# First layer's attention: heads p and 4+p together in four steps, values stationary, probabilities scaled before they are turned

## The chip, the cores and the metric

The kernel runs on one core of a Trainium2 chip (trn2). The metric is the device time of one launch, in microseconds (us), as the median of three runs. TensorE (PE) multiplies matrices and writes PSUM; its weight loads are shown apart as PEld. VectorE (DVE), ScalarE (ACT) and GpSimd (POOL) work element by element; SyncE (SP) issues the DMAs. Each engine runs its own list of instructions in the order in which they are written, and the engines wait for each other on semaphores.

## The reference

256 tokens of 1024 features pass through two layers of one kind and one of another. Only the mixer of the first layer is touched:

```python
def even_mixer(y, w_in, w_out, sinks, lb, gnorm_w):
    qa, ka, va, qb, fb, ib, gb = jnp.split(y @ w_in, EVEN_SPLITS, axis=-1)
    qa, ka = rope(qa), rope(ka)             # 8 query heads of 64, 2 key/value heads of 64
    oa = chunk_band_attention(qa, ka, va, 2, None, sinks)
    ob = hgrn2(qb, fb, ib, gb, lb, gnorm_w)  # 4 heads of 128, recurrent over 8 blocks of 32 tokens
    return jnp.concatenate([oa, ob], axis=-1) @ w_out

# chunk_band_attention, with sinks, for query head h and key/value head h // 4
m = max(max(s), sink[h])
p = exp(s - m)
p = p / (sum(p) + exp(sink[h] - m))
o = p @ v
# hgrn2, from block to block
o = qd @ state
state = dec * state + ke.T @ vv
```

## The kernel before

**Weights.** The weights come as units of 128 x 1024 numbers. SP loads unit n into `raw` (L531), ACT rounds it to `hi` (`round_unit`, L617), DVE subtracts to get `lo` (`split_unit`, L1513), and TensorE multiplies hi*hi, hi*lo and lo*hi. `units(upto)` in the lists of ACT and DVE does this for all units up to a number; TensorE waits for `lo_done` in `wait_unit`. Every place at which a unit is split is written out by hand in the two lists.

**The stage that the change touches.** TensorE's loop L1242 to L1262 has eight steps, one for each attention head s. A step issues the scores of head s (`scores`, L1110, the keys' and queries' 64 rows as contraction, PSUM bank s % 2), a share of the filler (`fill`, L1187), the recurrence's products (`kv`, L1197), the mix of head s-1 (`mix`, L1133, turned probabilities stationary, 64 columns of values moving), and at last the turning of the probabilities of head s (`turn_probs`, L1122). The heads of key/value head 0 (s below 4) all lie on array rows 0 to 63, the others on rows 64 to 127.

**Filler.** `fill` computes three products of the same layer and of the memory (hg, mk, mv): 12 pieces i of 8 steps each, a step being 3 matmuls of 256 columns. Pieces 2p and 2p+1 are the two token tiles of pair p and share bank 6; `fill_copy(p)` on ACT empties it (`fill_evac`) before the next pair starts, and pair p uses units 2p (k 0 to 3) and 2p+1 (k 4 to 7) of the filler. `FILLED` says which piece each step reaches.

**Recurrence.** `kv(b)` (b 0 to 6) writes bank 7 and waits for `stated` b, that is for DVE's `new_state(b-1)` (L1801 for b = 0, L1805 after). `hgrn(t)` (L1204, L1207) then computes the output of token tile t in bank 7; ACT squares it (`head_square`, L667), DVE sums (`head_sums`, L1612), POOL takes the root (L560, L562), DVE scales (`hgrn_scale`, L1617, L1813) and signals `hgrn_out`. `hgrn(1)` waits for `hgrn_out` 1.

**Softmax.** DVE adds the window and takes the maximum (`scores_max`, L1642, L1646), ACT takes the exponentials with their sum (`exps`, L677), TensorE turns, DVE copies (`probs_copy`, L1654), TensorE mixes. The sinks enter once, after the last head (L1835, L815, L1842), and the outputs of all heads are scaled at the end (`scale_outputs`, L1662 to L1665) and turned (`even_turn(0, t)`, L1079) for the output projection `even_part` (L1220). Its parts u = 0 to 3 use the recurrence's output, u = 4 to 7 the attention's.

**Before and after the loop.** ACT and DVE enter it with two filler units split. Head s on ACT runs `exps`, then the units up to `FILLED[s+1] + 2`, then the copies of the pairs that end there; DVE runs the maxima, one `new_state`, then the same units.

## Time and profile before

| what | value |
|---|---|
| median of 3 runs | 1078.79 us (1078.71 to 1078.82) |
| profiled execution, span | 1077.9 us |
| PE busy, all of the span | 1069.0 us (99%) |
| DVE busy | 749.4 us (70%) |
| ACT busy | 600.6 us (56%) |
| POOL busy | 108.8 us (10%) |
| DMA, mean | 178 GB/s |

The profiled execution's span is 0.9 us below the median, so a difference worked out on the trace carries over to the median. An engine that is busy for the whole span sets the time; the others matter where it waits for them. A timeline row gives the start in us, the duration from the first start to the last end, engine, line, operation, output and inputs. Neighbouring matmuls overlap in these durations, so what a piece of work costs TensorE is read from its start to the start of what follows.

### The profile page before, as it was taken

How to read it: one execution, taken by the hardware profiler on the slowest of the kernel's cores; microseconds unless marked ns; L12 is line 12 of the kernel's file. 1: busy time of each engine (PE TensorE's matmuls, PEld its weight loads, DVE VectorE, ACT ScalarE, POOL GpSimd, SP SyncE). 2: the span in 40 equal slices, each digit the busy share in tenths (PEclk: the TensorE clock that was granted, in tenths of full speed). 3: DMA queues.
4: the chain of work that ended last, by engine and by line, in shares of the span. 5: the costliest groups of instructions: out<-in, count | busy, mean ns of one | idle time of the engine just before them, and what ended most of it. 6: DMA issues, size and time to landing. Idle time of an engine off the chain costs nothing.

```text
span 1077.9 us, 16723 instructions
## 1 busy us (share of the span) xinstructions
PE 1069.0 (99%) x6712; PEld 947.7 (88%) x6712; DVE 749.4 (70%) x1109; ACT 600.6 (56%) x994; POOL 108.8 (10%) x127
## 2 busy tenths in 40 slices
PE   8999999999999999999999999999999999999998
PEld 6988889888888899898888888889999989888887
DVE  6876585998846566768988555957655885766751
ACT  5754465776734454557766444446544744655640
POOL 4020000131100000001111000221000000211100
PEclk9999999999999999999999999999999999999999
DMA  7851356665664755267656656464433546665661
GB/s 269 292 177 58 118 183 239 196 195 174 205 195 157 265 166 152 97 201 237 194 174 216 195 174 216 148 215 146 120 117 118 158 153 214 184 194 173 216 194 40
DMA packets 56957, 192.29 MB, mean 178 GB/s; under 512 B 6832, under 2 KB 9776, under 8 KB 56880
## 3 DMA queue, kind: packets, MB, share of 16 engines
q1 hardware_dynamic: 56880, 191.22, 55.5%
q8 instruction: 53, 0.87, 0.3%
q14 instruction: 24, 0.20, 0.1%
HBM read 190.15 MB, written 1.05 MB: 177 GB/s over the span
## 4 chain that ended last, share of the span: by engine, by line
PE 94%; DVE 2%; POOL 1%; ACT 1%; issue 0%; DMA 0%; SPq 0%; DVEq 0%; ACTq 0%; POOLq 0%
PE ps L958 28%; PE ps L1047 19%; PE ps L1039 15%; PE ps L1048 10%; PE ps L1313 5%; PE ps L1187 3%; PE ps L1133 3%; PE ps L1110 2%; PE ps L1374 2%; PE ps L1122 1%; PE ps L1059 1%; PE ps L1172 1%; DVE lo L1513 1%; POOL hr L562 1%; PE ps L1079 1%; PE ps L1197 1%
## 5 line engine op out<-in xcount | busy, mean ns | idle before, releaser
L1513 DVE TENSOR_TENSOR lo<-raw,hi 128x1024 fp32r<-128x1024 f32 (+2 forms) x347 | 429.2, 1262 | 87.6 <-ACT hi L617 84.7
L617 ACT ACTIVATE hi<-raw 128x1024 fp32r<-128x1024 f32 (+2 forms) x347 | 347.5, 1037 | 91.2 <-DMA raw<-in_weights 84.8
L1047 PE MATMUL ps<-y_both,hi 128*128 128x512 f32 x912 | 310.7, 389 | 0.0
L1048 PE MATMUL ps<-y_both,lo 128*128 128x256 f32 x912 | 251.8, 276 | 0.0
L1047 PEld LDWEIGHTS ps<-y_both,hi 128*128 128x128 f32 x912 | 171.2, 188 | 35.4
L1048 PEld LDWEIGHTS ps<-y_both,lo 128*128 128x128 f32 x912 | 171.2, 188 | 0.0
L1039 PE MATMUL ps<-y_both,hi 128*128 128x256 f32 x912 | 161.3, 280 | 0.8 <-DVE lo L1513 0.8
L1039 PEld LDWEIGHTS ps<-y_both,hi 128*128 128x128 f32 x912 | 138.5, 189 | 1.5 <-DVE lo L1513 1.0
L1039 PE MATMUL ps<-y_both,lo 128*128 128x256 f32 x456 | 126.7, 278 | 0.0
L958 PE MATMUL ps<-hi,y_both 128*128 128x512 f32 x352 | 94.1, 382 | 2.9 <-DVE lo L1513 1.4
L958 PE MATMUL ps<-hi,h_hi 128*128 128x512 f32 x294 | 91.0, 391 | 0.0
L958 PE MATMUL ps<-lo,h_hi 128*128 128x512 f32 x294 | 90.7, 390 | 0.0
L958 PE MATMUL ps<-hi,h_lo 128*128 128x512 f32 x294 | 90.6, 389 | 0.0
L1039 PEld LDWEIGHTS ps<-y_both,lo 128*128 128x128 f32 x456 | 85.9, 188 | 0.0
L571 POOL TENSOR_TENSOR h_lo<-pt,h_hi 128x256 fp32r<-128x256 f32 x66 | 51.7, 784 | 313.0 <-ACT h_hi L687 313.0
L958 PEld LDWEIGHTS ps<-hi,y_both 128*128 128x128 f32 x352 | 63.6, 188 | 16.8 <-DVE lo L1513 2.2
L1680 DVE TENSOR_TENSOR pr<-ps,pr 128x512 f32<-128x512 f32 x57 | 39.3, 689 | 47.4 <-ACT pr L701 47.3
L701 ACT ACTIVATE pr<-ps 128x512 f32<-128x512 f32 x57 | 33.8, 594 | 66.9 <-PE ps L1048 66.9
L958 PEld LDWEIGHTS ps<-hi,h_lo 128*128 128x128 f32 x294 | 55.2, 188 | 11.7
L958 PEld LDWEIGHTS ps<-lo,h_hi 128*128 128x128 f32 x294 | 55.2, 188 | 11.6
L958 PEld LDWEIGHTS ps<-hi,h_hi 128*128 128x128 f32 x294 | 54.7, 188 | 11.1
L677 ACT ACTIVATE pr<-sc,neg 128x128 f32<-128x128 f32 x80 | 35.5, 445 | 49.8 <-DVE neg L1646 49.8
(291 smaller groups left out, 1383.0 us busy)
## 6 DMA issues: line engine op xcount, KB each, us to landing
raw<-in_weights SPq DMA_DIRECT2D x331, 512.0 KB, 4.2
gain<-in_gains SPq DMA_DIRECT2D x10, 512.0 KB, 8.1
raw<-in_weights SPq DMA_DIRECT2D x8, 384.0 KB, 7.1
bias<-in_rel SPq DMA_DIRECT2D x16, 128.0 KB, 2.2
raw<-in_weights SPq DMA_DIRECT2D x8, 256.0 KB, 2.6
mem_x<-in_mem SPq DMA_DIRECT2D x2, 512.0 KB, 9.9
h<-in_x SPq DMA_DIRECT2D x2, 256.0 KB, 2.8
h<-in_x SPq DMA_DIRECT2D x1, 512.0 KB, 5.9
```

Of the source, the lines that this page charges most:

```text
L571: pool.tensor_tensor(h_lo[:, j, :], pt[:, j % 2, :S], h_hi[:, j, :].bitcast(F32), ALU.subtract).then_inc(h_lo_done, 1)
L617: act.activation(hi_at(n)[:, :w], raw_at(n)[:, :w], ACT.Copy).then_inc(hi_done, 1)
L677: e = act.activation(pr[:, a % 2, c], src, ACT.Exp, bias=neg[:, col, t:t + 1], accum_out=tot[:, col, t:t + 1])
L701: act.activation(pr[:, j % 2, :].rearrange("p (a b) -> p a b", a=2), both_parts(j, 1), ACT.Copy).then_inc(low_part, 1)
L958: mm = pe.matmul(ps[:, base + 2 * t + half_, :cw], x[:, k, tok], w(n)[:, c0:c0 + cw], start=i == 0 and k == 0, stop=i == 2 and n == last(n ...
L1039: mm = pe.matmul(dst, w(n)[:, at], x(k), start=first and k == 0, stop=final and k == nk - 1)
L1047: pe.matmul(dst, hi_at(n)[:, at], y_both[:, :, k, :], start=k == 0, stop=False)
L1048: mm = pe.matmul(dst[:, 0:S], lo_at(n)[:, at], y_hi[:, k, :], start=False, stop=k == KD - 1)
L1133: mm = pe.matmul(place(stage, hh, t), pt[:, a % 2, i * P:(i + 1) * P], v(kt), start=kt == 0, stop=kt == kts[-1])
L1313: mm = pe.matmul(lead_place(layer, j, t), x[:, k, tok], w(n)[:, c], start=k == 0 and i == 0, stop=k == KD - 1 and i == 2)
L1513: dve.tensor_tensor(lo_at(n)[:, :w], raw_at(n)[:, :w], hi_at(n)[:, :w].bitcast(F32), ALU.subtract).then_inc(lo_done, 1)
L1680: dve.tensor_tensor(p, both_parts(j, 0), p, ALU.add).then_inc(summed, 1)
```

## The change

The eight steps become four. Step p does heads p and 4+p: their scores are issued one after the other, one on array rows 0 to 63 and one on 64 to 127; their probabilities are turned together; and `mix_pair` has the values stationary (64 columns, the two heads on different column halves) and the turned probabilities moving (256 and 128 columns), with the result already feature by feature in bank 4 or 5. So the scaling is moved ahead of the turning: ACT computes each head's sink term right after its exponentials, DVE adds and inverts (`sinks_inverse`), ACT multiplies the probabilities (`scale_probs`). The turning of the outputs and their scaling go; `heads_hi` and `heads_lo` take the mixed heads from PSUM. The filler's pieces are dealt 1, 3, 5, 8, 12, the seven `kv` three, three and one to the steps, and `hgrn(0)` and `hgrn(1)` lie in steps 2 and 3. Weight columns, output rows and sinks are laid out in the new order of heads, and counts of semaphores follow. The list of what ACT and DVE do in a step is written anew. The core of the diff:

```diff
-    heads = np.concatenate([r(HD * x, HD * x + HD) for p in range(4) for x in (p, 4 + p)] + [r(512, 768)])
+    paired = np.concatenate([r(HD * x, HD * x + HD) for p in range(4) for x in (p, 4 + p)])
+    heads = np.concatenate([paired, r(512, 768)])
     two = np.concatenate([np.concatenate([r(P * j, P * j + P), FF + r(P * j, P * j + P)]) for j in range(KF)])
     pairs = np.concatenate([np.concatenate([r(P * j, P * j + P), D + r(P * j, P * j + P)]) for j in range(8)])
     even, odd, w2 = a["even_w_in"][0], a["odd_w_in"][0], a["w_in_2"][0]
     u = rows(even, heads) + columns(even, r(1280, 1792)) + columns(even, r(768, 1280))
     i = even[:, 1792:2304].reshape(4, 2, P, 512).transpose(0, 2, 1, 3).reshape(4, P, UNIT)
     u += list(i) + by_k(even[:, 2304:2816]) + by_k(a["w_mem_kv_2"][0])
-    out = rows(a["even_w_out"][0], r(D))
+    out = rows(a["even_w_out"][0][np.concatenate([paired, r(512, D)])], r(D))
...
-        FILLED = [1, 2, 3, 4, 5, 6, 8, 10, 12]
-        EVEN_TURN = ((3, 2), (2, 7))
+        FILLED = [1, 3, 5, 8, 12]
+        EVEN_TURN = (2, 7)
...
+        def turns_before(stage):
+            return 4 * stage - 2 * (stage > 2)
+        def mixed_bank(p):
+            return ps[:, 4 + p // 2 % 2, :].rearrange("p (a b) -> p a b", b=S)
...
+            def scale_probs(stage, hh):
+                a, col = ATT[stage][0] + hh, COLUMN[stage] + hh
+                act.wait_ge(sums_inverted, a + 1)
+                for t in range(NT):
+                    c = slice(P * t, P + S * t)
+                    e = act.activation(pr[:, a % 2, c], pr[:, a % 2, c], ACT.Copy, scale=rec[:, col, t:t + 1])
+                e.then_inc(probs_scaled, 1)
...
-            def even_hi(kh, t, i):
-                act.wait_ge(turned, 4 * 2 + i)
-                act.activation(token_half(y_hi, kh, t), split4(bank(EVEN_TURN[kh][t])), ACT.Copy).then_inc(y_hi_done, 1)
-            for hh in range(8):
-                exps("a", hh)
-                if hh == 7:
-                    even_hi(1, 0, 1)
-                units(FIRST["fill"] + FILLED[hh + 1] + 2)
-                for p in range(6):
-                    if FILLED[hh] < 2 * p + 2 <= FILLED[hh + 1]:
-                        fill_copy(p)
-                if hh == 3:
+            def even_hi(t):
+                act.wait_ge(turned, 4 * 2 + t + 1)
+                act.activation(token_half(y_hi, 1, t), split4(bank(EVEN_TURN[t])), ACT.Copy).then_inc(y_hi_done, 1)
+            def heads_hi(e):
+                act.wait_ge(mixed, 4 * e + 4)
+                act.activation(y_hi[:, 2 * e:2 * e + 2, :], mixed_bank(2 * e), ACT.Copy).then_inc(y_hi_done, 1)
+            def fill_units(to, copied):
+                units(FIRST["fill"] + to)
+                for p in copied:
+                    fill_copy(p)
+            for p in range(4):
+                for hh in (2 * p, 2 * p + 1):
+                    exps("a", hh)
+                    act.activation(esnk[:, hh, :], neg[:, hh, :], ACT.Exp, bias=rows_in[:, hh:hh + 1]).then_inc(act_sink, 1)
+                if p == 3:
+                    act.wait_ge(o_made, 2)
+                    head_square(1, split4(bank(7)), 4, P)
+                    heads_hi(0)
+                if p == 0:
+                    fill_units(4, [0])
+                elif p == 1:
+                    fill_units(6, [1])
+                elif p == 2:
+                    fill_units(8, [2])
+                else:
+                    even_hi(0)
+                    fill_units(11, [4])
+                scale_probs("a", 2 * p)
+                scale_probs("a", 2 * p + 1)
+                if p == 1:
                     act.wait_ge(fill_evac, 2)
                     act.activation(whole(hg), whole(hg), ACT.Silu).then_inc(hg_evac, 1)
                     act.activation(warm[:, :], half[:, 8:16], ACT.Exp)
-                if hh in (4, 6):
-                    t = (hh - 4) // 2
-                    act.wait_ge(o_made, t + 1)
-                    head_square(t, split4(bank(7)), 4, P)
-            act.wait_ge(maxed, 8)
-            act.wait_ge(dve_sink, 1)
-            act.activation(esnk, snk, ACT.Exp).then_inc(act_sink, 1)
-            even_hi(1, 1, 2)
+                if p == 2:
+                    act.wait_ge(o_made, 1)
+                    head_square(0, split4(bank(7)), 4, P)
+                    fill_units(9, [3])
+                fill_units((5, 7, 10, 14)[p], [5] if p == 3 else [])
+            even_hi(1)
             units(FIRST["even_out"] + 5)
-            even_hi(0, 0, 3)
-            even_hi(0, 1, 4)
+            heads_hi(1)
...
-                    g, p = hh // 4, hh % 4
+                    g, p = hh % 2, hh // 2
...
-                pe.wait_ge(powed, a + 1)
+                if stage == "a":
+                    pe.wait_ge(probs_scaled, a + 1)
+                else:
+                    pe.wait_ge(powed, a + 1)
                 if a >= 2:
                     pe.wait_ge(probs_copied, a - 1)
                 for i in range(4 if stage == "x" else 3):
                     mm = pe.transpose(ps[:, 2 + a % 2, i * P:(i + 1) * P], pr[:, a % 2, i * P:(i + 1) * P], ident[:, :])
                 mm.then_inc(probs_turned, 1)
+            def mix_pair(stage, p):
+                a = ATT[stage][0] + 2 * p
+                pe.wait_ge(probs_copied, a + 2)
+                dst = mixed_bank(p)[:, p % 2, :]
+                for kt in range(NT):
+                    for i in range(2):
+                        _, _, v = operands(stage, 2 * p + i)
+                        mm = pe.matmul(dst[HD * i:HD * i + HD, kt * P:S], v(kt), pt[:, (a + i) % 2, S * kt:S * kt + (S, P)[kt]],
+                                       start=kt == 0, stop=kt == 1, skip_group_check=True)
+                        if kt == 1:
+                            mm.then_inc(mixed, 1)
...
-            def even_turn(kh, t):
-                turn_heads(xhat, t, 512 * kh, EVEN_TURN[kh][t], turned)
+            def even_turn(t):
+                turn_heads(xhat, t, 512, EVEN_TURN[t], turned)
...
-            for s in range(8):
-                scores("a", s)
-                if s == 6:
+            for p in range(4):
+                scores("a", 2 * p)
+                scores("a", 2 * p + 1)
+                if p == 3:
                     pe.wait_ge(hgrn_out, 1)
-                if s in (4, 6):
-                    pe.wait_ge(stated, 7)
-                    hgrn((s - 4) // 2)
-                steps = KD * (FILLED[s + 1] - FILLED[s])
-                cut = 0 if s == 7 else steps // 4
-                fill(FILLED[s], 0, cut)
-                if s < 4:
-                    kv(2 * s)
-                if s:
-                    mix("a", s - 1)
-                if s == 7:
-                    even_turn(1, 0)
-                fill(FILLED[s], cut, 6 * steps // 8)
-                if s < 3:
-                    kv(2 * s + 1)
-                fill(FILLED[s], 6 * steps // 8, steps)
-                turn_probs("a", s)
+                    hgrn(1)
+                steps = KD * (FILLED[p + 1] - FILLED[p])
+                cuts = [0, steps // 4, steps // 2, 3 * steps // 4, steps]
+                for i in range(4):
+                    fill(FILLED[p], cuts[i], cuts[i + 1])
+                    if i < (3, 3, 1, 0)[p]:
+                        kv(3 * p + i)
+                    if i == 1 and p == 2:
+                        pe.wait_ge(stated, 7)
+                        hgrn(0)
+                    if i == 0 and p:
+                        mix_pair("a", p - 1)
+                        if p == 3:
+                            even_turn(0)
+                if p == 3:
+                    pe.wait_ge(y_lo_done, 4 * 2 + 2)
+                turn_probs("a", 2 * p)
+                turn_probs("a", 2 * p + 1)
             pe.wait_ge(hgrn_out, 2)
-            even_turn(1, 1)
+            even_turn(1)
             pe.wait_ge(row_max, 8)
-            pe.wait_ge(y_lo_done, 9)
             even_part(0, 0)
-            mix("a", 7)
-            even_part(1, 0)
-            even_part(2, 0)
-            for t in range(NT):
-                pe.wait_ge(attended, t + 1)
-                even_turn(0, t)
-            even_part(3, 0)
+            mix_pair("a", 3)
+            for u in range(1, 4):
+                even_part(u, 0)
             pe.wait_ge(fill_evac, 6)
-            pe.wait_ge(y_lo_done, 10)
+            pe.wait_ge(y_lo_done, 4 * 2 + 3)
             even_part(0, 1)
-            pe.wait_ge(y_lo_done, 11)
             for u in range(4, 8):
+                if u == 6:
+                    pe.wait_ge(y_lo_done, 4 * 2 + 4)
                 mm = even_part(u, 0)
             mm.then_inc(tile_done, 1)
-            pe.wait_ge(y_lo_done, 12)
...
-            def even_lo(kh, t, i):
-                dve.wait_ge(y_hi_done, 4 * 2 + i)
-                dve.tensor_tensor(token_half(y_lo, kh, t), split4(bank(EVEN_TURN[kh][t])), token_half(y_hi, kh, t).bitcast(F32),
+            def even_lo(t):
+                dve.wait_ge(y_hi_done, 4 * 2 + t + 2)
+                dve.tensor_tensor(token_half(y_lo, 1, t), split4(bank(EVEN_TURN[t])), token_half(y_hi, 1, t).bitcast(F32),
                                   ALU.subtract).then_inc(y_lo_done, 1)
-            for hh in range(8):
-                scores_max("a", hh)
-                if hh < 4:
-                    new_state(2 * hh)
-                if hh in (5, 7):
-                    hgrn_scale((hh - 5) // 2)
-                if hh == 0:
-                    units(FIRST["fill"] + 3)
-                    new_state(1)
-                units(FIRST["fill"] + FILLED[hh + 1] + 2)
-                if hh in (1, 2):
-                    new_state(2 * hh + 1)
-                if hh == 7:
-                    even_lo(1, 0, 1)
-                    dve.wait_ge(maxed, 8)
-                    dve.tensor_tensor(snk, neg[:, 0:8, :], rows_in[:, 0:8].rearrange("p (a b) -> p a b", b=1).to_broadcast([P, 8, 2]),
-                                      ALU.add).then_inc(dve_sink, 1)
-                probs_copy("a", hh)
-                if hh in (4, 6):
-                    head_sums((hh - 4) // 2, 4, P)
-            dve.wait_ge(act_sink, 1)
-            dve.wait_ge(powed, 8)
-            link(dve.tensor_tensor(tot[:, 0:8, :], tot[:, 0:8, :], esnk, ALU.add))
-            even_lo(1, 1, 2)
+            def heads_lo(e):
+                dve.wait_ge(y_hi_done, 4 * 2 + (1, 4)[e])
+                dve.tensor_tensor(y_lo[:, 2 * e:2 * e + 2, :], mixed_bank(2 * e), y_hi[:, 2 * e:2 * e + 2, :].bitcast(F32),
+                                  ALU.subtract).then_inc(y_lo_done, 1)
+            def sinks_inverse(hh):
+                dve.wait_ge(act_sink, hh + 1)
+                link(dve.tensor_tensor(tot[:, hh, :], tot[:, hh, :], esnk[:, hh, :], ALU.add))
+                dve.reciprocal(rec[:, hh, :], tot[:, hh, :]).then_inc(sums_inverted, 1)
+            for p in range(4):
+                scores_max("a", 2 * p)
+                scores_max("a", 2 * p + 1)
+                units(FIRST["fill"] + (3, 6, 8, 11)[p])
+                for i in range((3, 3, 1, 0)[p]):
+                    new_state(3 * p + i)
+                    if i == 0:
+                        sinks_inverse(2 * p)
+                        sinks_inverse(2 * p + 1)
+                if p == 3:
+                    sinks_inverse(6)
+                    sinks_inverse(7)
+                    heads_lo(0)
+                    even_lo(0)
+                    head_sums(1, 4, P)
+                    hgrn_scale(1)
+                if p == 2:
+                    units(FIRST["fill"] + 9)
+                    head_sums(0, 4, P)
+                units(FIRST["fill"] + (5, 7, 10, 14)[p])
+                if p == 2:
+                    hgrn_scale(0)
+                probs_copy("a", 2 * p)
+                probs_copy("a", 2 * p + 1)
             units(FIRST["even_out"] + 3)
-            scale_outputs("a", lambda t: xhat[:, t, 0:512])
+            even_lo(1)
             units(FIRST["even_out"] + 5)
-            even_lo(0, 0, 3)
-            even_lo(0, 1, 4)
+            heads_lo(1)
```

## Rows read from the trace of the kernel before

**Rows 1.** The page: the chain that ended last, by engine.

```profile
PE 94%; DVE 2%; POOL 1%; ACT 1%; issue 0%; DMA 0%; SPq 0%; DVEq 0%; ACTq 0%; POOLq 0%
```

**Rows 2.** TensorE's waits over the whole span: whom for, us, times, longest.

```profile
PE ps L958 <- DVE lo L1513: 1.4, 1, 1.4
...
PE ps L1059 <- DVE xhat L1551: 0.3, 1, 0.3
```

**Rows 3.** The loop: length, busy PE, PEld, DVE, ACT, POOL, granted clock, DMA.

```profile
73.00:135.00 62.00, 62.00 (x493) 53.71 (x493) 37.84 (x91) 27.56 (x56) 4.91 (x6) 1.00 0.28 86
```

**Rows 4.** TensorE's timeline, one step of one head.

```profile
79.52 0.49 PE L1122 MATMUL ps<-ident,pr 128*128 128x128 f32 x3
79.94 0.92 PE L1110 MATMUL ps<-k_t,q_t 64*128 64x128 f32 x4
80.79 0.38 PE L1187 MATMUL ps<-hi,y_both 128*128 128x256 f32 x1
...
81.69 1.15 PE L1197 MATMUL ps<-hv,kend 32*128 32x128 f32 x8
82.77 0.88 PE L1133 MATMUL ps<-va,pt 128*128 128x64 f32 x6
83.46 0.36 PE L1187 MATMUL ps<-hi,y_both 128*128 128x256 f32 x1
```

**Rows 5.** TensorE's timeline in the second layer, where two heads go together.

```profile
376.28 0.93 PE L1110 MATMUL ps<-k_t,q_t 64*128 64x128 f32 x8
377.14 0.50 PE L1039 MATMUL ps<-y_both,hi 128*128 128x256 f32 x2
...
379.99 1.03 PE L1122 MATMUL ps<-ident,pr 128*128 128x128 f32 x6
380.77 0.48 PE L1039 MATMUL ps<-y_both,hi 128*128 128x256 f32 x2
```

**Rows 6.** The chain, one head of `hgrn(1)`: start, us, what.

```profile
119.48 0.36 PE ps L1207 x8
```

**Rows 7.** TensorE's timeline where the outputs are turned.

```profile
140.66 1.04 PE L1079 MATMUL ps<-ident,xhat 128*128 128x128 f32 x8
141.51 0.72 PE L1220 MATMUL ps<-hi,y_both 128*128 128x512 f32 x2
```

**Rows 8.** Timeline of DVE and ACT in the first step.

```profile
74.24 0.35 DVE L1642 CUSTOM_DVE_ANT_0 sc<-ps,window,rows_in 128x128 f32<-128x128 f32 x1 [3.09 <-PE ps L1110]
...
75.24 0.40 ACT L677 ACTIVATE pr<-sc,neg 128x128 f32<-128x128 f32 x1 [5.97 <-DVE neg L1646]
...
76.14 1.04 ACT L617 ACTIVATE hi<-raw 128x1024 fp32r<-128x1024 f32 x1
```

**Rows 9.** Timeline: a state, a split, and from the squares' sums to `hgrn_out`.

```profile
93.68 1.12 DVE L1805 SCALAR_TENSOR_TENSOR state_own<-state_own,he,ps 128x128 f32<-128x128 f32 x4 [1.11 <-PE ps L1197]
...
98.79 1.22 DVE L1513 TENSOR_TENSOR lo<-raw,hi 128x1024 fp32r<-128x1024 f32 x1
...
109.80 0.69 DVE L1612 TENSOR_REDUCE hs<-rot 128x4 f32<-128x512 f32 x1 [0.23 <-ACT rot L667]
...
111.97 0.69 DVE L1617 TENSOR_TENSOR xhat<-ps,hr 128x512 f32<-128x512 f32 x1 [0.61 <-POOL hr L562]
...
112.70 0.69 DVE L1813 TENSOR_TENSOR xhat<-xhat,hg 128x512 f32<-128x512 f32 x1
```

**Rows 10.** ACT's timeline: tables and silu, from first to last, a copy.

```profile
98.72 1.28 ACT L807 ACT_TABLE_LOAD   x1
...
102.38 0.21 ACT L808 ACTIVATE warm<-half 128x8 f32<-128x8 f32 x1
...
108.68 0.60 ACT L791 ACTIVATE mk<-ps 128x512 f32<-128x512 f32 x1 [2.98 <-PE ps L1187]
```

**Rows 11.** TensorE's first matmuls, after idle, and some behind them.

```profile
1.13 5.09 PE L1143 MATMUL ps<-ones 128*128 128x256 f32 x12 [1.13 <-POOL ones L573]
...
7.72 1.46 PE L1143 MATMUL ps<-ones 128*128 128x256 f32 x6
```

More of the change, by code:

```diff
@@ L210, in lay_out @@
         "g_q_moba_2", "g_k_moba_2", "g_q_fox_2", "g_k_fox_2", "g_q_mem_2", "g_k_mem_2")])[None]
-    rows_in = a["even_sinks"]
+    rows_in = a["even_sinks"].reshape(1, 2, 4).transpose(0, 2, 1).reshape(1, 8)
     forget_b = np.zeros((P, 1), np.float32)
@@ L275, in build @@
         rec = sb("rec", [20, 2])
-        snk, esnk = top[:, 8:16, :], tot[:, 8:16, :]
+        esnk = tot[:, 8:16, :]
         ncum = sb("ncum", [S])
@@ L371, in build @@
         probs_turned, probs_copied, mixed = sem("probs_turned"), sem("probs_copied"), sem("mixed")
+        sums_inverted, probs_scaled = sem("sums_inverted"), sem("probs_scaled")
         attended = sem("attended")
@@ L380, in build @@
         mk_ready, mk_turned, mk_evac = sem("mk_ready"), sem("mk_turned"), sem("mk_evac")
-        dve_sink, act_sink = sem("dve_sink"), sem("act_sink")
+        act_sink = sem("act_sink")
         roped, a_turned, a_evac = sem("roped"), sem("a_turned"), sem("a_evac")
@@ L405, in build @@
         COLUMN = {"a": 0, "c": 0, "m": 0, "f": 8, "x": 16}
-        ATTENDED = {"a": 0, "c": 2, "m": 6, "f": 8, "x": 10}
+        ATTENDED = {"c": 0, "m": 4, "f": 6, "x": 8}
         def third_heads(k):
@@ L646, in turned_hi @@
                     for kh in range(2):
-                        act.wait_ge(turned, 4 * stage + 2 * t + kh + 1)
+                        act.wait_ge(turned, turns_before(stage) + 2 * t + kh + 1)
                         act.activation(token_half(dst, kh, t), split4(bank(base + 2 * t + kh)), ACT.Copy).then_inc(y_hi_done, 1)
@@ L826, in out_hi @@
             def out_hi(kh, t):
-                act.wait_ge(turned, 4 * 5 + 2 * kh + t + 1)
+                act.wait_ge(turned, turns_before(5) + 2 * kh + t + 1)
                 act.activation(out_y(0, kh, slice(t * P, (t + 1) * P)), split4(bank(2 + t)), ACT.Copy).then_inc(y_hi_done, 1)
@@ L1389, in _ @@
                     if j == 6:
-                        pe.wait_ge(attended, ATTENDED["c"] + 2)
+                        pe.wait_ge(attended, 2)
                     mix("c", 2 * j - 4)
@@ L1580, in norms_between @@
             def norms_between(g, p, base, name, stage, turn_base):
-                dve.wait_ge(turned, 4 * stage)
+                dve.wait_ge(turned, turns_before(stage))
                 units(last(name) + RAW - TAIL)
@@ L1862, in _ @@
             dve.tensor_copy(v1[:, 1, :], two_banks(6)).then_inc(v_evac, 1)
-            dve.wait_ge(turned, 20)
+            dve.wait_ge(turned, turns_before(5))
             for j in range(9):
```

## The prediction, made before the change was built

> **What bounds the kernel now.** I read the page's chain first: TensorE carries 94% of it [rows 1]. Its waits over the whole span are the next view, because a change that regroups work can only add to them: the longest is 1.4 us, at the very start, and the one nearest to our stage is 0.3 us [rows 2]. In the loop from 73 to 135 us TensorE is busy for all 62.0 us, DVE for 37.8, ACT for 27.6, and the DMAs for 28% [rows 3]. So a microsecond less of TensorE's work is a microsecond less of time, but only if each split unit, state and maximum still comes before TensorE asks for it. The shares of DVE and ACT don't tell that; their order within a step does. I therefore lay the new order out step by step.
>
> **TensorE's work, part by part.** Scores of one head take 0.85 us (79.94 to 80.79) [rows 4]; in the second layer, where the two heads lie on different row halves, 8 matmuls take 0.86 (376.28 to 377.14) [rows 5]. Eight times 0.85 becomes four times 0.86: 3.4 us less. The mix of a head takes 0.69 (82.77 to 83.46) [rows 4], a pair 1.4. No row shows the new form. A matmul of 128 f32 columns in two passes costs about 0.21 (8 transposes of one pass in 0.85 [rows 7]), so a head has 384 columns, 0.64. If the column halves run together, a pair costs 0.64 and some 0.25 for changing over; if not, 1.5. I take 0.9, since a head's four column tiles of `hgrn(1)` take 0.36 for 8 matmuls that would need 0.85 one after another [rows 6]: 2.0 us less. The eight transposes of the outputs go, 0.85 [rows 7], and turning two heads at once is 0.78 (379.99 to 380.77) against 2 times 0.42 [rows 4, 5]: with one change-over less per pair 0.3 us. The seven `kv` (82.77 - 81.69 = 1.08 each [rows 4], 1.28 with change-overs) and all filler steps stay. In all TensorE has 6.5 us less to do.
>
> **The new order, from scores to scores.** Durations that recur: a filler step is 0.354 (its 3 matmuls start 0.118 apart); the first maximum starts 1.05 after the scores (their 0.92 [rows 4] and a latency); exponentials start 1.0 later (74.24 to 75.24) and take 0.90 (to 76.14) [rows 8]; a sink term on ACT 0.2 [rows 10]; `hi` 1.04 [rows 8]; `lo` 1.22 and a state 1.12 [rows 9], both with 1.1 from start to next start; a copy from PSUM 0.6 [rows 10]. The two exponentials with their sinks and the next `hi` end 5.3 after the step's start, and the `lo` 6.5.
> Step 0: DVE's list has `units(fill + 3)` ahead of `new_state(0)`, so the state is ready at 6.5 + 0.7 = 7.2. TensorE wants it for `kv(1)` at 0.96 + 1.42 + 1.18 + 1.52 + 0.09 = 5.2. Wait A: 2.1. Behind `kv(2)` the filler's k 4 to 7 of piece 2 need unit 3, and DVE splits that one only after `new_state(2)`, which itself waits for `kv(2)`: 1.1 + 1.2 + 0.1 from the end of `kv(2)`. Wait B: 2.35, whatever the pace.
> Step 1: the same chain with unit 5 and a full state gives 7.6 for `new_state(3)`; TensorE comes to `kv(4)` after 0.96 + 1.42 + 1.18 + 0.9 + 1.52 = 6.0. Wait C: 1.65. ACT then scales two heads (0.7 each, the two exponentials' activates without their sums) and runs silu between two table loads, 3.9 us (98.72 to 102.59) [rows 10], before it rounds unit 6. So DVE begins step 2's maxima 2.65 after its scores instead of 1.07.
> Step 2: pieces 5, 6, 7. Piece 6 starts a new pair in the middle of the filler and needs bank 6 empty, with nothing between to cover `fill_copy(2)`; ACT comes to it behind exponentials and unit 7, done at 2.65 + 1.0 + 2 x 1.1 + 0.95 + 0.6 = 7.4. TensorE is there at 0.96 + 2.12 + 1.18 + 0.9 + 0.71 = 5.9. Wait D: 1.6. `hgrn(0)` then waits 0.4 for `new_state(6)` (E).
> Step 3: `hgrn(1)` stands right behind the scores and needs `hgrn_out` 1. That hangs on the end of step 2's filler: copy 0.56, unit 9 on ACT 1.04 and on DVE 1.2, then the two scalings 1.42 (111.97 to the end of the 0.69 at 112.70) [rows 9], 4.3 in all. TensorE needs for its turning and scores 0.78 + 0.86. Wait F: 2.6. Piece 10 starts in mid-step as well and wants unit 10, which ACT rounds only behind `even_hi(0)`, and bank 6, emptied 0.65 after the last matmul of piece 9. Wait G: 0.65. Four steps later, 1.4 us, it wants unit 11. DVE splits that at the end of a row of nine: two inverses (0.8, an estimate from the add and reciprocal of small tiles at about 0.2 each), `heads_lo` and `even_lo` (0.6 each), the squares' sums 0.69, POOL's root until 111.97 (2.17 from the sums' start [rows 9], so 1.48), the scalings 1.42, the split 1.22: 6.8 after unit 10's split, which itself ends as piece 9 does. Wait H: 6.8 - 0.75 - 1.4 = 4.65.
> Behind the loop I find nothing late: unit 13 and the mix's inputs come a microsecond or more ahead, and ACT and DVE have 8 us from `mix_pair(3)` to the part that needs its output. The norm of the first token tile is close to a tie there, 0 to 0.5.
>
> **The sum.** A to H are 2.1 + 2.35 + 1.65 + 1.6 + 0.4 + 2.6 + 0.65 + 4.65 = 16.0. After each a first matmul may start some 0.1 slower, which I put at 0.5 in all with the tie. 16.0 + 0.5 - 6.5 = +10.0. The traced execution stood 0.9 under the median, and since everything behind the stage is TensorE's own work at 1.00 clock, nothing gives the ten back: 1078.8 + 10.0 = 1088.8 us.
> Two costs are hidden or not by these waits. ACT's scaling is 16 activates, 5.6 us, and eight sink terms, 1.6; DVE's sixteen small operations 3.2. They lie in idle time except where named above (C, D, H). The change adds waits to their lists: behind ACT's wait for an inverted sum stand the next roundings and bank 6's copy, behind DVE's wait for a sink term the next state and the probabilities' copies, and TensorE waits for those; D and H count that. TensorE's new wait for `heads_lo` and `even_lo` ahead of turning heads 3 and 7 is met, as both come before the split of unit 11. The DMAs are at 28% in the loop [rows 3], and SP's list keeps its order; the layout of weights is made on the host.
>
> **A rule of the skill.** The rows say that packing pays on TensorE (8 matmuls in the time of 4 [rows 4, 5]) and that bank 6 is then the thing waited for (D, G). The Trainium skill, "TensorEngine Tiling (Array Packing)", section PSUM Bottleneck, says that packing speeds up TensorE and not the emptying of PSUM; by it alone D and G would be 1.4 us rather than 2.3, since it counts only the copy.
>
> **The rivals.** (1) The waits are covered and only the lighter TensorE shows: 1078.8 - 6.5 = 1072.3. For it speaks that TensorE never waits now [rows 3]; against it that B, F and H follow from one engine's own order, whose links wait for TensorE itself. 4 in 100.
> (2) The waits are there but less than half as long, for instance because H is broken by an earlier split: about -1 to +2 us, 1078 to 1081. It would need half of the eight listed waits to be misread. 4 in 100.
> (3) The two halves don't run together. Each scores pair is 0.85 longer and each mix 0.6; of that, what lies ahead of A, C and D is swallowed: about 3 us more, 1092. The second layer's rows speak against it for scores [rows 5], none for the mix. 6 in 100.
> (4) TensorE's clock falls in the longest wait, H, and perhaps F. The granted clock is 1.00 through the loop, the upper level (2.4 GHz), with TensorE always busy [rows 3]. The first matmuls of the launch, after an idle start, take 5.09 / 12 = 0.42 each and the later ones 1.46 / 6 = 0.24 [rows 11]: half speed over some 5 us, so a fall costs up to 2.5: 1091.3, with both 1093.8. It decides once an idle stretch is long enough; none before was over 1.4 us [rows 2], so no row tells where that is. The Trainium skill, "TensorE: Matmul & The Clock Gate", section Why this matters for your kernels, warns that an idle gap between bursts puts TensorE back to the lower clock. No row here shows that, and I give it 20 in 100 for the length of H.
> (5) The change doesn't do what it says, e.g. the mix's `kt` order makes four separate changes of the column half, 0.3 more per pair: within the forecast's range.
>
> **How the numbers follow.** The forecast, waits as laid out and the clock held, has 66 in 100, rival 3 six, rival 4 twenty, 1 and 2 four each. Its own range is the sum of the unknowns: the mix from 0.75 to 1.5 (of four, two count: -0.3, +1.2), inverses and scalings +-0.7 in H and D, a latency of +-0.05 on some thirty links, 1.5. That gives 1086.3 to 1091.3. The wanted range takes in one fall of the clock and leaves out rivals 1 and 2 and the far end of 4: 1085.8 to 1092.3. A measurement here can tell 0.2%, 2.2 us, from no change. Faster by that is rival 1 and a little beside it, 0.05; within it is rival 2, 0.04; slower 0.91.
>
> **What would show it.** In the changed kernel's view of TensorE's waits: a wait of `kv(1)` for the first state, of the filler for `lo` after `kv(2)` (2.3 us) and in step 3 (4 to 5 us), of `hgrn(1)` for the scaling of the first tile (2.6 us), and two for ACT's copy out of bank 6. Scores of a pair should span 0.86 and `mix_pair` 0.9; the granted clock should stay 1.00. The stage from the first scores to the first matmul of the lead (L1313), 87.6 us now, should be 97 to 98. If B, F or H is missing, I have misread an order and the prediction is wrong by its size; if the stage matches and the total doesn't, something behind it moved.

## The result and the profile after

| what | before | after |
|---|---|---|
| median | 1078.8 us | 1098.4 us |
| ratio, 95% interval | 1 | 1.0176 (1.0154 to 1.0198) |
| executions | 1078.7 to 1079.4 us | 1094.9 to 1100.5 us |
| granted clock, mean over the span | 1.00 | 0.984 to 0.994 |
| profiled execution, span | 1077.9 us | 1098.6 us |
| profiled execution, first scores to the first matmul of the lead | 87.55 us | 107.12 us |

The change makes the kernel 1.8% slower, 19.6 us. I had forecast 10.0 us slower, with a range up to 1092.3: right in sign, too small by half. Executions of the changed kernel differ by more than those of the one before, and go with the granted clock: the two at 1100.4 and 1100.5 us have 0.986 and 0.984, the others 0.992 and 0.994.

The page of the changed kernel, from its parts on engines, slices of the span and the chain:

```profile
PE 1074.7 (98%) x6688; PEld 951.0 (87%) x6688; DVE 746.9 (68%) x1120; ACT 607.0 (55%) x1017; POOL 108.9 (10%) x127
...
PEclk9998889999999999999999999999999999999999
...
PE 90%; DVE 4%; ACT 2%; POOL 1%; issue 1%; DMA 1%; SPq 0%; DVEq 0%; ACTq 0%; POOLq 0%
```

TensorE's share of the chain is 90% where it was 94% [rows 1], and the granted clock is below 0.9 in slices 4 to 6, which lie from 82 to 165 us and so in the stage. TensorE's own waits in the stage (whom for, us in total, times, longest):

```profile
PE ps L1240 <- DVE lo L1563: 6.4, 2, 4.0
PE ps L1257 <- DVE xhat L1863: 2.7, 1, 2.7
PE ps L1250 <- DVE hf L1851: 1.9, 1, 1.9
PE ps L1250 <- DVE hk L1855: 1.4, 1, 1.4
PE ps L1240 <- ACT mk L810: 1.4, 1, 1.4
PE ps L1240 <- ACT mv L810: 0.7, 1, 0.7
PE ps L1096 <- DVE xhat L1601: 0.5, 1, 0.5
```

Before, this list held one wait of 0.3 us in the same stretch [rows 2], the norm's, which is 0.5 now (L1096). L1240 is the filler, L1250 `kv`, L1257 `hgrn`. Busy time by stretch of the stage (length; busy PE, PEld, DVE, ACT, POOL; granted clock; DMA; GB/s):

```profile
74.00:84.00 10.00, 8.08 (x58) 7.17 (x59) 5.17 (x20) 7.05 (x18) 0.00 (x0) 0.93 0.34 107
84.00:94.00 10.00, 7.65 (x39) 6.61 (x37) 4.45 (x8) 0.00 (x0) 0.00 (x0) 0.56 0.00 0
94.00:127.00 33.00, 27.96 (x228) 23.48 (x228) 17.23 (x54) 18.29 (x41) 3.73 (x4) 1.00 0.31 96
127.00:138.00 11.00, 10.43 (x66) 7.87 (x68) 3.17 (x13) 3.32 (x12) 0.00 (x0) 0.54 0.01 1
138.00:147.00 9.00, 5.78 (x48) 5.05 (x45) 4.53 (x10) 6.36 (x10) 1.21 (x2) 1.00 0.36 118
147.00:156.00 9.00, 7.50 (x42) 7.50 (x43) 3.76 (x5) 0.37 (x1) 0.00 (x0) 0.62 0.12 24
156.00:181.00 25.00, 24.48 (x120) 19.71 (x118) 20.96 (x27) 15.70 (x24) 1.11 (x2) 1.00 0.53 183
```

The same view had a single 1.00 for the whole loop [rows 3]. Here it is near 0.5, the lower of the two levels (1.2 GHz), in most of 84 to 94, of 127 to 138 and of 147 to 156 us. In narrower windows the low stretches lie from 82.6 to 92.8, from 127.0 to 137.2 and from 147.4 to 154.3 us. TensorE is busy for 10.43 of the 11 us from 127, so this is not idleness: the matmuls themselves take about twice as long. In the timeline of TensorE, the scores, a `kv` at the low clock, the end of wait B, and the mix:

```profile
73.88 0.93 PE L1147 MATMUL ps<-k_t,q_t 64*128 64x128 f32 x8
...
84.63 2.07 PE L1250 MATMUL ps<-hv,kend 32*128 32x128 f32 x8
89.06 0.58 PE L1240 MATMUL ps<-hi,y_both 128*128 128x256 f32 x1 [2.35 <-DVE lo L1563]
...
96.62 0.87 PE L1173 MATMUL ps<-pt,va 128*64 128x256 f32 x8
97.42 0.39 PE L1240 MATMUL ps<-hi,y_both 128*128 128x256 f32 x1
```

The scores of two heads span 0.93 us as in the second layer [rows 5], the mix of a pair takes 97.42 - 96.62 = 0.80 us against 0.69 for one head [rows 4], and the `kv` at 84.63 takes 2.07 us where it took 1.15 [rows 4].

**Where the 19.6 us are.** The stage from the first scores to the lead, before and after, in the view of the stretches above:

```profile
73.17:160.72 87.55, 87.29 (x617) 74.81 (x617) 60.88 (x123) 44.32 (x82) 6.02 (x8) 1.00 0.37 115
...
73.88:181.00 107.12, 92.00 (x594) 77.51 (x593) 59.27 (x134) 51.08 (x105) 6.05 (x8) 0.87 0.29 94
```

TensorE was busy for 87.29 of 87.55 us before, and for 92.00 of 107.12 after: its idle time grew by 14.9 us. The version without waits (experiment 4) has the same matmuls at full clock and is busy for 80.44 us, 6.85 less than before. So the changed kernel's TensorE was busy for 92.00 - 80.44 = 11.6 us more than its work needs at full clock. -6.85 + 14.9 + 11.6 = +19.6. The low stretches alone give the same 11.6: they last 27.3 us, TensorE is idle in 4.0 of these, and half of the other 23.3 is lost, 3.9, 4.8 and 2.9 us in the three. The idle time had been forecast (16.0) and the lighter work too (6.5); the 11.6 us of half speed had not, except as a rival at 2.5 to 5.

This ledger is that of the profiled execution, 1100.4 us, 2 us above the median. Part of these 2 us lies outside the stage, in a fourth low stretch, which stands behind a wait of 1.4 us that the kernel before has too [rows 2] and bears at a clock of 1.00:

```profile
PE ps L995 <- DVE lo L1563: 1.4, 1, 1.4
...
14.00:18.00 4.00, 4.00 (x16) 3.48 (x17) 2.36 (x4) 0.31 (x1) 0.00 (x0) 0.57 0.91 367
```

### The profile page after: what moved, and what is told of

Same layout as the page of the kernel before. It is cut to its first block, busy times and chain, and to the rows that moved or that the text cites. A ratio compares the mean times of both kernels' runs of the same rounds, so it can differ in the third digit from the quotient of the medians.

```text
span 1098.6 us, 16704 instructions
## 1 busy us (share of the span) xinstructions
PE 1074.7 (98%) x6688; PEld 951.0 (87%) x6688; DVE 746.9 (68%) x1120; ACT 607.0 (55%) x1017; POOL 108.9 (10%) x127
## 4 chain that ended last, share of the span: by engine, by line
PE 90%; DVE 4%; ACT 2%; POOL 1%; issue 1%; DMA 1%; SPq 0%; DVEq 0%; ACTq 0%; POOLq 0%
PE ps L995 27%; PE ps L1084 19%; PE ps L1076 14%; PE ps L1085 9%; PE ps L1363 5%; PE ps L1186 2%; PE ps L1240 2%; PE ps L1424 2%; PE ps L1147 2%; PE ps L1162 1%; DVE lo L1563 1%; PE ps L1096 1%; PE ps L1225 1%; PE ps L1273 1%; POOL hr L572 1%
## 5 line engine op out<-in xcount | busy, mean ns | idle before, releaser
L995 PEld LDWEIGHTS ps<-hi,h_lo 128*128 128x128 f32 x294 | 55.2, 188 | 11.6
L995 PEld LDWEIGHTS ps<-lo,h_hi 128*128 128x128 f32 x294 | 55.2, 188 | 11.6
```

The costliest lines, as they stand in the source:

```text
L995: mm = pe.matmul(ps[:, base + 2 * t + half_, :cw], x[:, k, tok], w(n)[:, c0:c0 + cw], start=i == 0 and k == 0, stop=i == 2 and n == last(n ...
```

## The experiments

Theory one, the forecast's with its rival 4: eight waits in TensorE's list, made by the order of ACT's and DVE's work, and a clock that falls behind them and costs much more than I had priced. Theory two: the excess is something that the ledger left out, work, latency, or too much load on ACT and DVE, and the clock only shows it.

**1. TensorE kept busy in its waits, too much of it.**

```diff
+            def busy(n):
+                for _ in range(n):
+                    pe.matmul(ps[:, 5, S:2 * S], ones[:, 0:P], ones[:, :], start=True, stop=True, skip_group_check=True)
...
+                    busy({(2, 4): 10, (6, 0): 5, (10, 0): 2, (10, 4): 19}.get((i, k), 0))   # in fill
+                busy({1: 8, 4: 6}.get(b, 0))                                               # in kv
+                    busy(11)                                                               # ahead of hgrn(1)
```

> The changed kernel with extra matmuls of ones (256 columns, into the unused half of bank 5) put ahead of seven of its waits: 8 before kv(1), 10 before the filler's unit 3, 6 before kv(4), 5 and 2 before the pairs that start in mid-step, 11 before hgrn(1), 19 before the filler's unit 11. The waits end when they ended, TensorE is busy in them. Theory (the ledger of waits is right and the excess over it is TensorE's clock, which falls after waits): granted clock 1.00 through the stage and 1087 to 1089 us, 10 us less than the changed kernel. Rival (the clock is only a symptom, the excess is work or latency that the ledger left out): within 2 us of the changed kernel's 1098.

Measured: 1099.5 us, ratio 1.0186 (1.0171 to 1.0201), granted clock 1.00 in every execution. This is the rival's number, but not for the rival's reason: the extra matmuls were mis-sized. The timeline where ten of them stand in for wait B:

```profile
85.62 4.58 PE L1231 MATMUL ps<-ones 128*128 128x256 f32 x20
89.86 0.47 PE L1245 MATMUL ps<-hi,y_both 128*128 128x256 f32 x1
```

Ten take 89.86 - 85.62 = 4.24 us, 0.42 each, twice what I had set. 61 of them are 25.9 us of work in place of the waits: 1079.3 - 6.85 + 25.9 = 1098.3, which is the time within 1.2 us, without any clock in it. So it says only that the clock holds when TensorE has no gaps; whether that pays had to be seen with the right number.

**2. The same, with half as many.** The numbers are 5, 3, 1, 9 in `fill`, 4 and 3 in `kv`, 6 ahead of `hgrn(1)`.

> As the first run of extra matmuls, but half as many: one of 256 f32 columns of ones took 0.43 us there at full clock (20 instructions in some 4.5 us), not the 0.22 that I had counted, so the 61 of them were 26 us of work in 15 us of waits. Now 4 ahead of kv(1), 5 ahead of the filler's unit 3, 3 ahead of kv(4), 3 and 1 ahead of the mid-step pairs, 6 ahead of hgrn(1), 9 ahead of the filler's unit 11: 31, 13 us. Theory (the ledger's waits, and the clock for the rest): granted clock 1.00 and 1087 to 1089 us, some 10 below the changed kernel. Rival (waits were sized right by chance and the excess is something else): 1096 or more.

Measured: 1089.1 us (1088.6 to 1089.6), ratio 1.0088 (1.0072 to 1.0105), clock 1.00. That is the theory's case, at the upper end of its 1087 to 1089. Busy time over the stage and what lies around it:

```profile
66.00:171.00 105.00, 103.94 (x721) 87.55 (x720) 65.22 (x142) 53.03 (x110) 6.05 (x8) 1.00 0.35 109
```

TensorE is busy for 99% of this stretch, part of it with work that nobody needs, and the kernel is 9 us faster than with idle waits. That separates the two costs: +9.4 us over the kernel before of the same comparison are waits less work saved (forecast: +10.0), and 1.76% - 0.88% = 0.88% of the time, 9.5 us, is the clock. Of the seven waits three still show, each with 0.2 to 0.3 us, and in the other four the extra matmuls may outlast the wait, so the waits' part is 9.4 us at most. That part lies within the noise of the comparison (1.8 us to either side) of the ledger's 10.0, and nothing is left that theory two is needed for.

**3. Units split earlier.**

```diff
+            units(FIRST["fill"] + 4)                      # ACT and DVE, ahead of the loop
...
+                    units(FIRST["fill"] + 12)             # ACT, step 3, ahead of the wait for o_made
-                units(FIRST["fill"] + (3, 6, 8, 11)[p])   # DVE
+                units(FIRST["fill"] + (3, 6, 8, 12)[p])
-                units(FIRST["fill"] + (5, 7, 10, 14)[p])  # ACT alike
+                units(FIRST["fill"] + (6, 7, 10, 14)[p])
```

> The changed kernel with units split earlier on ACT and DVE: four before the loop instead of two, the sixth at the end of step 0, unit 11 ahead of the sums' inverses in step 3. Theory (order of splits makes the waits A, B, C and H): these four go, D, F and G stay, 4.5 us of idle time; 1078.8 - 6.5 + 4.5 = 1077 if the clock holds, 1082 if it falls after the 2.6 us of F. Rival (the waits come from too much work on ACT and DVE, whatever the order): they move to other places, and the time stays above 1090.

Measured: 1081.65 us (1079.8 to 1084.1), ratio 1.0021 (1.0012 to 1.0031), granted clock 0.994 to 0.998. TensorE's waits in the stage:

```profile
PE ps L1259 <- DVE xhat L1866: 2.7, 1, 2.7
PE ps L1242 <- ACT mk L811: 1.7, 1, 1.7
PE ps L1242 <- ACT mv L811: 0.7, 1, 0.7
```

A, B, C and H are gone, F, D and G stand, 5.1 us in all. Those less the 6.85 us of work saved would be 1.8 us faster than before; it is 2.3 slower, which leaves 4 us. The granted clock of the ten executions, 0.994 to 0.998 with 0.997 in the middle, accounts for some 3 of them. In the profiled execution, a cheap one (1080.9 us), the one fall stands behind F, which ends at 117.96:

```profile
120.00:123.40 3.40, 3.40 (x25) 2.41 (x26) 1.03 (x6) 3.40 (x12) 0.00 (x0) 0.50 0.01 2
```

It costs 1.7 us there. ACT and DVE do the same work as in the changed kernel: the order made the waits, not the load.

**4. All waits covered.** Parts of the edit:

```diff
+            units(FIRST["fill"] + 4)                      # ACT and DVE, ahead of the loop
...
                 cuts = [0, steps // 4, steps // 2, 3 * steps // 4, steps]
+                if p == 2:
+                    cuts = [0, 8, 12, 18, 24]             # TensorE: kv, mix, turning where a pair of steps ends
+                if p == 3:
+                    cuts = [0, 16, 20, 26, 32]
...
-                    units(FIRST["fill"] + 9)              # DVE, step 2
                     head_sums(0, 4, P)
+                    hgrn_scale(0)
...
-                    even_lo(0)                            # DVE, step 3
                     head_sums(1, 4, P)
                     hgrn_scale(1)
+                    even_lo(0)
-                units(FIRST["fill"] + (3, 6, 8, 11)[p])
+                units(FIRST["fill"] + (4, 6, 8, 12)[p])   # and 5, 7, 10 behind the sums' inverses
...
+                    fill_copy(2)                          # ACT, step 2, alone: unit 7 is rounded in step 1 now
+                    units(FIRST["fill"] + 12)             # ACT, step 3, ahead of the wait for o_made
```

> The same products in the same four steps, with the order of ACT's and DVE's work written anew, and on TensorE the kv, the mix and the turning laid where a filler pair ends, so that no wait of the ledger is left. Theory (TensorE's work is 6.5 to 7 us less and nothing else bounds the stage): 1072 us, granted clock 1.00. Rival (ACT's added scaling and DVE's added small operations don't fit): waits of a microsecond and more in steps 1 and 2, 1078 or above.

Measured: 1072.7 us (1071.8 to 1073.2), ratio 0.9935 (0.9919 to 0.9952), clock 1.00. This beats both kernels. Its one wait, and the stage from the first scores to the lead:

```profile
PE ps L1102 <- DVE xhat L1611: 0.5, 1, 0.5
...
72.87:153.77 80.90, 80.44 (x594) 68.42 (x593) 57.36 (x133) 49.10 (x103) 6.04 (x8) 1.00 0.39 125
```

80.90 us against 87.55: the 6.65 us that the change takes off TensorE's path, where the forecast had 6.5 for the work. ACT is busy for 49.1 of these 80.9 us and DVE for 57.4, so the added scalings fit. The change itself is worth having; its hand-written order, with the clock's falls that came of it, was what cost 26 us.

**5. One wait alone, 3.4 us.** In the kernel before, TensorE waits after the scores of head 2 for nine dependent memsets on the idle POOL.

```diff
+            pool.wait_ge(scored, 3)
+            for i in range(9):
+                if i:
+                    pool.wait_ge(held, i)
+                pool.memset(ncum[:, :], 0.0).then_inc(held, 1)
...
                 scores("a", s)
+                if s == 2:
+                    pe.wait_ge(held, 9)
```

> The kernel before with one wait added: after the scores of head 2 TensorE waits for nine dependent memsets on the idle POOL, some 3.7 us; nothing else is changed. Theory (a wait of this length costs itself and then a stretch of half speed of about 10 us, as behind the waits of the changed kernel): 1078.8 + 3.7 + 5 = 1087 to 1088 us, granted clock 0.5 over some 10 us behind it. Rival (half speed only comes from several waits together): 1082 to 1083, clock 1.00.

Measured: 1085.4, 1086.2, 1093.2, 1093.7 and 1093.8 us, against 1079.25 before, ratio 1.0104 (1.0070 to 1.0137). The wait in the profiled execution (1093.8), and busy time with the granted clock around it:

```profile
PE ps L1193 <- POOL ncum L594: 3.4, 1, 3.4
...
88.00:92.00 4.00, 0.63 (x3) 0.27 (x2) 1.17 (x6) 1.93 (x5) 2.80 (x9) 0.92 0.00 0
92.00:112.00 20.00, 20.00 (x82) 17.67 (x83) 7.13 (x20) 6.18 (x10) 1.19 (x1) 0.50 0.18 53
112.00:116.00 4.00, 4.00 (x19) 3.34 (x18) 0.56 (x1) 0.18 (x1) 1.57 (x2) 0.59 0.00 0
116.00:120.00 4.00, 4.00 (x41) 2.72 (x41) 1.94 (x6) 1.93 (x5) 0.00 (x0) 1.00 0.00 0
```

The clock is at the lower level from shortly before 92 until about 115 us, over 23 us in which TensorE is never idle. The price is the 3.4 us of the wait and 10 to 11 more in three executions, and 3 to 4 more in the two others. I had forecast 10 us of half speed and one price, 1087 to 1088: a single wait does bring the low clock, but neither execution had that price.

**6. One wait, 1.9 us**, the same with five memsets.

> The kernel before with the same added wait after the scores of head 2, of five memsets instead of nine, some 1.9 us, the length of the wait after which the changed kernel's clock fell first. Theory (one wait of that length can bring the lower clock by itself, though not in each execution): between 1081 and 1092, most likely two kinds of executions, some at 1081 and some 5 or more above. Rival (it needs several waits close together): all at 1081, clock 1.00.

Measured: 1084.85, 1090.0, 1090.2 and 1090.7 us against 1079.7, ratio 1.0087 (1.0064 to 1.0111). The cheapest of them was profiled:

```profile
PE ps L1193 <- POOL ncum L594: 1.9, 1, 1.9
...
88.00:90.00 2.00, 0.20 (x1) 0.00 (x0) 1.06 (x5) 0.64 (x3) 1.51 (x5) 1.00 0.00 0
90.00:92.00 2.00, 1.90 (x8) 1.68 (x9) 0.00 (x0) 1.30 (x3) 0.04 (x1) 0.56 0.00 0
92.00:96.00 4.00, 4.00 (x19) 3.78 (x19) 2.26 (x5) 0.00 (x0) 0.00 (x0) 0.50 0.00 0
96.00:98.00 2.00, 2.00 (x14) 1.87 (x13) 0.00 (x0) 0.00 (x0) 0.00 (x0) 0.73 0.31 31
```

A single wait as long as A (1.92 us in the changed kernel) is enough, and none of the four executions is at the 1081 of a held clock. Here the lower clock lasts for nearly 7 us, from about 90.2 to 97.1, and costs 3; in the other three it must have lasted longer, for 8 to 9 us are lost beyond the wait, with a granted clock of 0.990 over the span instead of 0.997.

**7. One wait, 1.2 us**, the same with three memsets.

> The kernel before with the added wait after the scores of head 2 made of three memsets, some 1.0 us. The wait of 1.9 us cost 5 to 11 us, that of 3.4 us 7 to 15. Theory (below some length the clock holds): all executions at 1080.5, 1.0 above the kernel before, clock 1.00. Rival (any wait in this stage, whose TensorE load is thin at its small matmuls, can tip it): some executions 3 us or more above that.

Measured: 1081.3 us as the median of ten, against 1079.65, ratio 1.0031 (1.0009 to 1.0053). TensorE's wait in the profiled execution, the cheapest (1080.0):

```profile
PE ps L1193 <- POOL ncum L594: 1.2, 1, 1.2
```

Seven lie between 1080.0 and 1081.5, with the clock at 1.00 in all but one: they pay the wait. One has 1084.2 (clock 0.997) and two have 1089.2 and 1090.2 (0.990), 8 to 9 us beyond a wait of 1.2. The rival holds, if only in 3 of 10.

**8. One wait, 1.9 us, in the first feed-forward**, where matmuls have 256 and 512 columns throughout. The memsets wait for `unit_used` of column 9, TensorE waits ahead of column 10.

> The kernel before with a wait for five dependent memsets, 1.9 us, in the first feed-forward (ahead of its column 10), where TensorE has only dense matmuls with 256 to 512 columns before and behind. Theory (the price hangs on the wait alone): 5 to 11 us above the kernel before, as in the attention stage. Rival (the price hangs on how thin TensorE's work is around it, too): 1.9 to 3 us above, clock 1.00.

Measured: 1082.7 us (1081.2 to 1084.0) against 1079.65, ratio 1.0035 (1.0022 to 1.0047), clock 0.998 to 1.00. TensorE's wait there:

```profile
PE ps L1054 <- DVE pr L1689: 1.9, 1, 1.9
```

It is as long as that of experiment 6 (the trace puts it down to the later of two semaphores) and costs 3.1 us with it, against 10.4. So the price hangs on where the wait stands, too. The 1.2 us beyond the wait don't go with the granted clock (the slowest execution, 1084.0, has 1.00) and stay unexplained. What it is about the place isn't settled: in the attention stage TensorE runs short matmuls on 32 and 64 rows with changes between them, and I didn't vary that alone.

**9. The scaling first.**

```diff
                     head_sums(0, 4, P)
+                    hgrn_scale(0)
                 units(FIRST["fill"] + (5, 7, 10, 14)[p])
-                if p == 2:
-                    hgrn_scale(0)
```

> The changed kernel with one swap in DVE's list: the scaling of the recurrence's first tile goes ahead of the split of unit 9, so that the wait of hgrn(1) for it (2.7 us) goes. Theory (order alone makes that wait; behind it lie 10 us at half speed, 5 us lost): no wait of hgrn(1), 1098.4 - 2.7 - 5 = 1091. Rival (the clock falls anyway, from the other waits): 1095 to 1096. Second rival (the scaling is late for another reason): no change.

Measured: 1092.2 us (1091.8 to 1092.9), ratio 1.0118 (1.0103 to 1.0133), 0.58% or 6.3 us less than the changed kernel. What is left of F, and two stretches:

```profile
PE ps L1257 <- DVE xhat L1863: 0.5, 1, 0.5
...
102.00:108.00 6.00, 6.00 (x32) 5.45 (x32) 3.25 (x7) 2.96 (x4) 2.51 (x2) 0.54 0.00 0
126.00:132.00 6.00, 6.00 (x68) 4.67 (x62) 3.06 (x13) 3.20 (x12) 0.00 (x0) 1.00 0.12 48
```

F is down from 2.7 to 0.5 us, and the stretch behind it stands at 1.00. But now the clock is low from 102 to 108, behind wait C, where the changed kernel's profiled execution had kept it. Wait D, which the edit doesn't touch, is down from 1.35 to 0.69 us with this low stretch just ahead of it; that the slower TensorE gave ACT the time is likely, not shown. In the stage the profiled execution has 3.5 us less idle time and 3.0 us less busy time than the changed kernel's. So the falls are not tied one to one to the waits: each wait is a chance of one.

**10. The mix's order**, in the version without waits.

```diff
-                for kt in range(NT):
-                    for i in range(2):
+                for i in range(2):
+                    for kt in range(NT):
```

> The version without waits, with the four matmuls of a pair's mix in another order: both of one head, then both of the other, instead of alternating between the column halves. Theory (the halves run together only where neighbouring matmuls lie on different halves): a pair takes 1.1 to 1.3 us instead of 0.80, four pairs cost 1.2 to 2 us more, 1074 to 1075. Rival (the order doesn't matter, the array takes each half's matmuls as they come): 1072.7.

Measured: 1073.1 us, ratio 0.9941 (0.9926 to 0.9956), the same as with the alternating order. The mix in its timeline:

```profile
87.34 0.88 PE L1179 MATMUL ps<-pt,va 128*64 128x256 f32 x8
88.15 0.39 PE L1246 MATMUL ps<-hi,y_both 128*128 128x256 f32 x1
```

88.15 - 87.34 = 0.81 us. The two heads' matmuls run together although both of one head are issued first, so rival 5 is out with its 0.3 us per pair.

## Why the prediction was right and where it failed

**TensorE's work.** 6.5 us less was forecast, 6.65 came out on the path (80.90 against 87.55). The scores' pair was 0.86, as read in the second layer [rows 5]. The mix, for which no row stood, was 0.80 against the 0.9 taken, at the lower end of its bounds; the row on the recurrence's column tiles [rows 6] was the right one to lean on. Rival 3 (the halves don't run together) is out. ACT's sixteen scalings took 5.95 us where 5.6 was written, and don't show in the time once the order is right.

**The waits.** Forecast and measured: A 2.1 and 1.92, B 2.35 and 2.35 (6.4 - 4.04), C 1.65 and 1.41, D 1.6 and 1.35, F 2.6 and 2.70, G 0.65 and 0.69, H 4.65 and 4.04; E doesn't show as an idle row of its own. Their sum of 14.5, or 14.9 with the small gaps, stands against 16.0. H came out shorter because of two terms of its own: DVE's row behind unit 10's split took 6.4 us (142.1 to 148.5) instead of 6.8, with 0.5 instead of 0.8 for the two inverses, and the four filler steps ahead of the wait took 1.7 instead of 1.4. The clock has no part in it: experiment 9's step 3 ran at 1.00 until H, and its H is as long:

```profile
142.15 0.58 PE L1240 MATMUL ps<-hi,lo 128*128 128x256 f32 x1 [4.05 <-DVE lo L1563]
```

D and G, for which the copy out of bank 6 alone would have given 1.4 us, measured 2.04 together against 2.25: the order of ACT's list counted. Each was where the order of the lists had put it, and each of those that an experiment took out (A, B, C, H by splitting earlier, F by one swap but for 0.5 us, all by the new order) went. With TensorE kept busy in them the kernel was 9.4 us slower than the one before; the sum without the clock had said 10.0. The range around that sum was too narrow by its own terms: upwards they add to 1.2 + 0.7 + 1.5 = 3.4, which is 1092.2 and not 1091.3. Rivals 1 and 2 are out; TensorE's 100% in the loop before [rows 3] was no cover.

**The step that failed** is the end of the sum: "since everything behind the stage is TensorE's own work at 1.00 clock, nothing gives the ten back". Nothing gave it back, but the clock did not stay at 1.00 in the stage. I had rival 4 and took it as one fall behind H and perhaps one behind F, at up to 2.5 us each, and gave it 20 in 100. It was mis-sized in three ways. Its price: I took the length of a low stretch from the launch's first matmuls, about 5 us [rows 11], and from their durations alone, since the profile prints a granted clock of 1.00 for its first 5 us; the stretches of the changed kernel are 7 to 10 us and cost 2.9 to 4.8, and the one behind a single wait of 3.4 us was 23. Where it strikes: I put it behind the longest waits, but a wait of 1.9 us tips the clock in each of four executions, and one of 1.2 us in three of ten. Its number: each of the waits is a chance, and the profiled execution had three falls in the stage, behind A, F and H. So rival 4 at its far end, 1093.8, was still short of 1098.4. The Trainium skill, "TensorE: Matmul & The Clock Gate", section Why this matters for your kernels, warns that idle gaps between bursts of matmuls bring the clock down. The runs agree that a gap can do it, but they show it behind shorter gaps than the page warns of, 1.9 and 1.2 us, and not behind each: here the measurement decides.

What should have warned me is in the rows: the view of waits before held nothing above 1.4 us in 1078 [rows 2], so the trace could not show what a longer one does, and a range on a cost that no row bounds from above has to be wider. The 11.6 us of the three falls would have closed the gap, but their length stands in no row from before; only the runs have it.

## What to carry to other kernels

When a change regroups the work of the busiest engine, lay out the lists of all engines from step to step: each of the seven waits that showed was readable ahead to 0.3 us or so, save the longest (0.6 off). Count an idle gap of TensorE above a microsecond not at its length but at that plus a chance of several us of half speed behind it; in the feed-forward, the one other place tried, that price was much smaller; where a gap can't be closed, useless matmuls in it, about as many as fill it, gave back 9.5 us here, and twice as many gave back nothing. And before a rewrite is dropped for being slower, look whether its work or its order is at fault: the same matmuls in another order went from 1.8% slower to 0.65% faster.

## What the runs showed of the hardware

- The clock stays low with TensorE fully busy: from 92 to 112 us TensorE was busy for 20.00 of 20.00 us at a granted clock of 0.50, and came back to 1.00 only at about 115 (experiment 5). The price of a fall differs between executions of one kernel: 3 to 11 us beyond the wait in that experiment, 3 to 9 in experiment 6.
- One wait of TensorE in this stage brought the low clock in four of four executions at 1.9 us and in three of ten at 1.2 us; a wait of 1.9 us in the feed-forward didn't clearly do so in any of six (0.998 to 1.00).
- An f32 matmul of 256 columns is two instructions and takes 0.42 us at full clock (10 in 4.24), against 0.118 from start to start for one of the filler's with rounded operands.
- Matmuls on different column halves overlap in either order of issue, 0.80 and 0.81 us for a pair that would be 1.28 one after the other, an estimate from 0.42 per 256 columns and 384 columns for each head.
- A multiplication by a per-row factor on ACT, SBUF to SBUF, costs as much as an exponential without its sum (0.39 us for 128 columns and 0.50 for 256, both); the sixteen of them kept ACT busy for 5.95 us, which doesn't show in the time once the order is right.
